# Gated linear attention in one kernel of two layers: chunks of 128 tokens with decays counted from the chunk's middle, in place of chunks of 64

## The reference

```python
def _gla_scan(q, k, v, log_a):            # chunks of c = 64 tokens, n = 4 of them
    cum = jnp.cumsum(log_a.reshape(b, h, n, c, dk), axis=3)
    q_t = q * jnp.exp(cum)
    k_t = k * jnp.exp(-cum)
    scores = jnp.where(mask, jnp.einsum('bhnid,bhnjd->bhnij', q_t, k_t), 0.0)
    o_inner = jnp.einsum('bhnij,bhnje->bhnie', scores, v)
    last = cum[..., -1:, :]
    kv = jnp.einsum('bhncd,bhnce->bhnde', k * jnp.exp(last - cum), v)
    decay = jnp.exp(last[..., 0, :])
    def step(state, inp):                 # state before a chunk, carried over the chunks
        kv_n, d_n = inp
        return d_n[..., None] * state + kv_n, state
    _, s_before = lax.scan(step, zeros, (kv, decay))
    o_cross = jnp.einsum('bhncd,bhnde->bhnce', q_t, s_before)
    return o_inner + o_cross
```

## Time and profile before

| | |
|---|---|
| time, median of 3 executions | 845.27 us (844.89 to 845.55) |
| span of the profiled execution | 843.8 us |
| median minus span | 1.5 us |
| PE busy | 829.3 us, 98% |
| PE weight loads | 701.4 us, 83% |
| DVE busy | 464.5 us, 55% |
| ACT busy | 428.4 us, 51% |
| DMA read | 147.85 MB, 178 GB/s over the span |

### The profile page before, as it was taken

The page is one execution under the profiler, slowest core; times in us unless marked ns, Lnnn a source line. Parts: engine busy times, 40 slices in busy tenths (PEclk is TensorE's granted clock), DMA queues, the critical chain, the costliest instruction groups (busy, mean ns, idle before and its releaser), DMA issues.

```text
span 843.8 us, 11480 instructions
## 1 busy us (share of the span) xinstructions
PE 829.3 (98%) x4084; PEld 701.4 (83%) x4084; DVE 464.5 (55%) x611; ACT 428.4 (51%) x616; POOL 50.2 (6%) x44
## 2 busy tenths in 40 slices
PE   6999999999999999999989999999999999999998
PEld 5898888888888888888869888888878888888886
DVE  2554497445375853654445635864653649546542
ACT  4864565456725543433347655663475345444441
POOL 6110000000000101000122000000000010010000
PEclk9999999999999999999989999999999999999999
DMA  8765764533543454565436656644354345546654
GB/s 343 251 230 190 240 215 150 174 125 126 175 150 125 147 178 150 193 206 198 156 117 227 246 186 227 198 150 150 125 175 147 128 147 162 176 139 204 194 186 140
DMA packets 41924, 150.67 MB, mean 179 GB/s; under 512 B 4752, under 2 KB 4880, under 8 KB 41744
## 3 DMA queue, kind: packets, MB, share of 16 engines
q1 hardware_dynamic: 40592, 145.25, 51.5%
q0 software_dynamic: 432, 2.88, 0.8%
q10 hardware_dynamic: 848, 1.83, 0.7%
HBM read 147.85 MB, written 2.10 MB: 178 GB/s over the span
## 4 chain that ended last, share of the span: by engine, by line
PE 96%; ACT 1%; issue 1%; DMA 1%; DVE 1%; SPq 0%; ACTq 0%; DVEq 0%
PE pair L357 84%; PE bank L388 4%; PE bank L637 1%; PE bank L611 1%; PE bank L500 1%; PE bank L679 1%; PE bank L669 1%; PE bank L592 1%; DMA raw<-stream 1%; PE bank L627 0%; PE bank L548 0%; PE bank L570 0%; PE bank L560 0%; ACT gate L731 0%; DVE lo L978 0%
## 5 line engine op out<-in xcount | busy, mean ns | idle before, releaser
L978 DVE TENSOR_TENSOR lo<-raw,hi 128x1024 fp32r<-128x1024 f32 (+3 forms) x266 | 307.3, 1178 | 213.1 <-ACT hi L713 209.2
L713 ACT ACTIVATE hi<-raw 128x1024 fp32r<-128x1024 f32 (+3 forms) x272 | 270.4, 1022 | 155.7 <-PE pair L357 132.5
L357 PE MATMUL pair<-lo,xT_hi 128*128 128x512 f32 (+1 forms) x768 | 296.9, 387 | 2.4 <-DVE xT_lo L995 2.4
L357 PE MATMUL pair<-hi,xT_hi 128*128 128x512 f32 (+1 forms) x768 | 296.0, 396 | 2.9 <-ACT xT_hi L747 2.6
L357 PE MATMUL pair<-hi,xT_lo 128*128 128x512 f32 (+1 forms) x768 | 296.9, 387 | 0.0
L357 PEld LDWEIGHTS pair<-lo,xT_hi 128*128 128x128 f32 x768 | 145.5, 189 | 30.2 <-issue 3.3
L357 PEld LDWEIGHTS pair<-hi,xT_hi 128*128 128x128 f32 x768 | 144.3, 189 | 30.4 <-ACT xT_hi L747 3.3
L357 PEld LDWEIGHTS pair<-hi,xT_lo 128*128 128x128 f32 x768 | 145.2, 189 | 28.5
L357 PE MATMUL pair<-hi,yT_hi 128*128 128x512 f32 (+1 forms) x304 | 116.7, 384 | 0.0
L357 PE MATMUL pair<-hi,yT_lo 128*128 128x512 f32 (+1 forms) x304 | 116.6, 383 | 0.0
L357 PE MATMUL pair<-lo,yT_hi 128*128 128x512 f32 (+1 forms) x304 | 116.5, 383 | 0.0
(11 more groups left out here) (138 smaller groups left out, 519.7 us busy)
## 6 DMA issues: line engine op xcount, KB each, us to landing
raw<-stream SPq DMA_DIRECT2D x272, 512.0 KB, 4.2
out<-x SPq DMA_DIRECT2D x8, 256.0 KB, 5.3
consts<-consts_in POOLq DMA_DIRECT2D x1, 1792.0 KB, 14.9
mats<-mats_in ACTq DMA_DIRECT2D x2, 576.0 KB, 3.5
x<-x_in POOLq DMA_DIRECT2D x2, 512.0 KB, 9.3
x<-x_in SPq DMA_DIRECT2D x1, 512.0 KB, 4.6
x<-x_in ACTq DMA_DIRECT2D x1, 512.0 KB, 9.0
consts<-consts_in ACTq DMA_DIRECT2D x1, 64.0 KB, 4.3
```

Source lines behind the costliest of these rows:

```text
L357: return nc.tensor.matmul(pair[a][m][:, 0:width], x_part[:, slots[i], m * P:(m + 1) * P], w_part[r][:, i * 512:i * 512 + width], start=(sl ...
L713: nc.scalar.activation(cut[0], cut[1], ACT.Copy).then_inc(rounded[r].sem, 1)
L978: nc.vector.tensor_tensor(cut[0], cut[1], cut[2].bitcast(F32), ALU.subtract).then_inc(split[r].sem, 1)
```

## The change

Mixer B works in chunks of 128 tokens, that is one chunk per token tile. The decays are counted from the middle of the chunk (token 64), not from its beginning, so that the exponents of q and k have both signs. In each direction only one state is left: what the first tile (of that direction) gives to the second. In detail:

- The triangular constants become `cum_f`, `cum_b` (signed sums around the middle), `keep_f`, `keep_b` (the masks), `after` and `before` over all 128 tokens, and a new one `halves` of 4 columns. The constants grow from 3584 to 3844 columns in the load that POOL issues.
- On PE the "rest of chunk" product is needed only for the tile that gives: 2 products of 256 columns where there were 4. New are 4 products of 2 columns (the decay from the tile's edge to its middle, `e_mid`).
- `k_dec` has no zeros beside blocks; a state update is 2 products of 256 columns per direction (heads in pairs): 4 where there were 16 of 128 columns, all at one place, where `outer_kv(0)` stood.
- The output of a tile is 4 products score by v and 4 products q by state with all 128 output rows, where there were 4 and 12 with 64 rows.
- ACT moves the state with 4 activations that scale by `e_mid`, where there were 12 copies; it evaluates 2 exponentials of 256 columns and 2 of 4 columns where there were 2 of 512.
- DVE makes `k_dec` in 2 instructions instead of 4; the 8 instructions that fold the state are gone. POOL no longer clears `k_dec`.

```diff
-                for m in range(MT):
-                    nc.tensor.matmul(bank[2 + m][:, 0:2 * P], const("after"), la[:, m, 0:2 * P],
+                for d, rest in enumerate(("after", "before")):
+                    gives, takes = d, 1 - d
+                    nc.tensor.matmul(bank[2 + d][:, 0:2 * P], const(rest), la[:, gives, d * 2 * P:(d + 1) * 2 * P],
                                      start=True, stop=True)
-                    nc.tensor.matmul(bank[2 + m][:, 2 * P:4 * P], const("before"), la[:, m, 2 * P:4 * P],
-                                     start=True, stop=True).then_inc(rem_filled.sem, 1)
+                    for f in range(2):
+                        at = d * 2 * P + f * P
+                        mm = nc.tensor.matmul(bank[2 + d][:, 2 * P + 2 * f:2 * P + 2 * f + 2],
+                                              la[:, takes, at:at + P], const("halves")[:, 2 * d:2 * d + 2],
+                                              start=True, stop=True)
+                    mm.then_inc(rem_filled.sem, 1)
...
                 pe.wait_ge(*v_b_ready.at(l, MT))
-                outer_kv(0)
-                granules(82)
-                outer_kv(1)
+                pe.wait_ge(*k_dec_ready.at(l, 2))
+                pe.wait_ge(*picked_ready.at(l, 2))
+                for d in range(2):
+                    for a in range(2):
+                        mm = nc.tensor.matmul(bank[2 + d][:, a * 2 * HD:(a + 1) * 2 * HD],
+                                              k_dec[:, d, a * P:(a + 1) * P],
+                                              v_b[:, d, a * 2 * HD:(a + 1) * 2 * HD], start=True, stop=True)
+                    mm.then_inc(kv_filled.sem, 1)
                 granules(85)
...
-                    for c in range(2):
-                        n = 2 * m + c
-                        for h in range(HEADS):
-                            for d in range(2):
-                                t = n - 1 if d == 0 else 2 - n
-                                if t < 0:
-                                    continue
-                                mm = nc.tensor.matmul(
-                                    bank[m][c * 64:(c + 1) * 64, h * HD:(h + 1) * HD],
-                                    q_heads[:, d, h // 2, m, h % 2, c * 64:(c + 1) * 64],
-                                    state[:, d, t, h // 2, :], start=False, stop=True,
-                                    skip_group_check=True)
+                    d = 1 - m
+                    for h in range(HEADS):
+                        mm = nc.tensor.matmul(
+                            bank[m][:, h * HD:(h + 1) * HD], q_heads[:, d, h // 2, m, h % 2, :],
+                            state[:, d, h // 2, (h % 2) * HD:(h % 2 + 1) * HD], start=False, stop=True,
+                            skip_group_check=True)
...
-                keep(0)
-                splits(84)
-                keep(1)
+                act.wait_ge(*e_mid_ready.at(l, 2))
+                for d in range(2):
+                    act.wait_ge(*kv_filled.at(l, d + 1))
+                    for a in range(2):
+                        nc.scalar.activation(state[:, d, a, :], bank[2 + d][:, a * 2 * HD:(a + 1) * 2 * HD], ACT.Copy,
+                                             scale=e_mid[:, d, a, 0:1]).then_inc(state_ready.sem, 1)
                 splits(84)
```

More of the change, by code:

```diff
@@ L84 @@
 CONSTS, nc_ = {}, 0
-for n_, w_ in (("ident", P), ("tri_f", P), ("tri_b", P), ("after", P), ("before", P),
+for n_, w_ in (("ident", P), ("cum_f", P), ("cum_b", P), ("keep_f", P), ("keep_b", P), ("after", P), ("before", P),
+               ("halves", 4),
                ("decay", HEADS * 3 * P), ("rcos", MT * HD // 2), ("rsin", MT * HD // 2),
@@ L177, in build @@
         sq_b = area(4096, 512)
-        e_rem = area(5120, 1024, "p (m d c) -> p m d c", m=MT, d=2)
+        e_rem = area(5120, 512, "p (d c) -> p d c", d=2)
         picked = area(7680, 512, "p (h i) -> p h i", h=HEADS)
-        state = area(6144, 1536, "p (d n a e) -> p d n a e", d=2, n=3, a=2)
+        state = area(6144, 1024, "p (d a e) -> p d a e", d=2, a=2)
+        e_mid = area(7168, 8, "p (d f o) -> p d f o", d=2, f=2)
         rq_rot = area(0, 1024, "p (n c) -> p n c", n=MT * HEADS)
@@ L590, in scores_b @@
                             pe.wait_ge(*e_rem_ready.at(l, d + 1))
+                            pe.wait_ge(*e_mid_ready.at(l, d + 1))
                         for f in range(2):
@@ L894, in _ @@
                 splits(76)
-                for m in range(MT):
-                    act.wait_ge(*rem_filled.at(l, m + 1))
-                    nc.scalar.activation(e_rem[:, m].rearrange("p d c -> p (d c)"), bank[2 + m][:], ACT.Exp,
+                for d in range(2):
+                    act.wait_ge(*rem_filled.at(l, d + 1))
+                    nc.scalar.activation(e_rem[:, d], bank[2 + d][:, 0:2 * P], ACT.Exp,
                                          scale=1.0 / GLA_TAU).then_inc(e_rem_ready.sem, 1)
+                    nc.scalar.activation(e_mid[:, d].rearrange("p f o -> p (f o)"), bank[2 + d][:, 2 * P:2 * P + 4],
+                                         ACT.Exp, scale=1.0 / GLA_TAU).then_inc(e_mid_ready.sem, 1)
                 splits(77)
@@ L902, in _ @@
                 splits(82)
[L904 to L915, removed]
-                                nc.scalar.activation(state[64 * i:64 * i + 64, d, t, :, :], cut[:, :, i, :], ACT.Copy
-                                                     ).then_inc(kv_kept.sem, 1)
-                keep(0)
-                splits(84)
-                keep(1)
+                act.wait_ge(*e_mid_ready.at(l, 2))
+                for d in range(2):
+                    act.wait_ge(*kv_filled.at(l, d + 1))
+                    for a in range(2):
+                        nc.scalar.activation(state[:, d, a, :], bank[2 + d][:, a * 2 * HD:(a + 1) * 2 * HD], ACT.Copy,
+                                             scale=e_mid[:, d, a, 0:1]).then_inc(state_ready.sem, 1)
                 splits(84)
@@ L1225, in _ @@
                 pick(1)
-                splits(82)
-                dve.wait_ge(*kv_filled.at(l, 2))
-                decay_k(1)
-                splits(84)
-                dve.wait_ge(*kv_kept.at(l, 12))
[L1232 to L1237, removed]
-                            nc.vector.scalar_tensor_tensor(
-                                out=state[:, d, t, a, :], in0=state[:, d, t - 1, a, :],
-                                scalar=e_pos[:, d, a, edge:edge + 1], in1=state[:, d, t, a, :],
-                                op0=ALU.mult, op1=ALU.add).then_inc(state_ready.sem, 1)
                 def head_squares(sq, m, squared, read):
@@ L1395, in shape_constants @@
     k, t = i[:, None], i[None, :]
-    same = (k // GLA_CHUNK) == (t // GLA_CHUNK)
     put("ident", k == t)
-    put("tri_f", same & (k <= t))
-    put("tri_b", same & (k >= t))
-    put("after", same & (k > t))
-    put("before", same & (k < t))
+    put("cum_f", 1.0 * ((k >= GLA_MID) & (k <= t)) - 1.0 * ((k < GLA_MID) & (k > t)))
+    put("cum_b", 1.0 * ((k < GLA_MID) & (k >= t)) - 1.0 * ((k >= GLA_MID) & (k < t)))
+    put("keep_f", k <= t)
+    put("keep_b", k >= t)
+    put("after", k > t)
+    put("before", k < t)
+    put("halves", np.concatenate([i[:, None] < GLA_MID] * 2 + [i[:, None] >= GLA_MID] * 2, axis=1))
     gamma = 1.0 - 2.0 ** (-5.0 - np.arange(HEADS))
```

49 lines of the change are left out of this document (16 added, 33 removed).

## The result

The changed kernel takes 834.7 us (834.22 to 834.93, 4 executions) against 845.25 (844.89 to 845.55, 4 executions) for the kernel before on the same chip. The ratio is 0.9882, 95% interval 0.987 to 0.9894. The forecast was 835.7.

The account below looks back on a forecast made before the run. PE was taken as the bound. From the 843.8 us span, -6.78 - 3.70 + 0.06 - 0.84 + 1.44 + 0.2 = -9.6 gave span 834.2, median 835.7 us; the 8-in-10 range was 833.3 to 838.0.

Parts of the forecast that it names:

- PE is the bound: Whole kernel: PE is busy 829.3 of 843.8 us, so PE time is kernel time unless PE must wait.
- Output products: Mixer B's output group on PE: falls from 6.96 to 3.57 us, -3.39 per layer, -6.78 in all.
- State updates: Mixer B on PE: two groups of 3.58 us become one of 1.73, -1.85 per layer, -3.70 in all.
- Rest of the chunk: Mixer B on PE: two wide products replaced by four 2-column ones at 0.224 us, +0.03 per layer, +0.06 in all.
- The old wait: Before granule 84: PE's wait for a late `lo` goes, -0.42 us per layer, -0.84 in all.
- The new wait: At granule 82: PE arrives before ACT's rounding, queued behind the state's move, is ready; +0.72 us per layer, +1.44 in all.
- One link: Within granule 82's wait: ACT starts its last two activations when direction 1 is filled, 1.92 us after the state update begins.
- Mixer B as a whole: All of mixer B's gains and losses taken together: -4.9 us per layer.
- The start: Kernel start: POOL's loads of x issued 0.95 us earlier compete with the first granule; +0.2 us, ends -0.3 and +0.5.
- such a microsecond: Start and layer boundary: the low-clock stretch's length may move by a microsecond with what stands before it.
- The reading that almost nothing of 64 rows runs side by side: Old output products: 64-row records cost 0.099 us each, against 0.056 by the skill's side-by-side rule.
- The rival of the clock: Mixer B: a longer wait at granule 82 lowers PE's clock in both layers, making the kernel slower, 849.1 us for example; chance 0.02.

Follow-up runs that it names:

- e1: Changed kernel with ACT's rounding of granule 82 placed ahead of the four activations that move the state: 833.15 us.
- e7: Changed kernel without its 2-column products, so the carried state has a wrong scale: 835.22 us.
- e3: Changed kernel with each 2-column product issued four times, 24 more in all: 844.8 us (838.98 to 846.93, 10 executions).
- e11: The same edit as e1, run beside the unedited changed kernel on one chip: 835.46 us against 835.25.
- e2: Changed kernel with half of `q_heads` cleared a second time before POOL's loads of x: 835.44 us.
- e9: Kernel before with 260 unused columns added to its constants: 845.61 us against 844.62, ratio 1.0008.
- e4: Changed kernel with each q by state product split into two of 64 output rows, upper and lower halves one behind the other: 836.9 us.
- e5: As e4, but the upper halves of all four heads first, then the lower ones: 838.52 us.
- e12: Kernel before with its 12 q by state products per tile reordered so neighbours lie in different halves where possible: 842.74 us against 844.62, ratio 0.9978.
- e6: Changed kernel with each state-update product cut into four of 64 moving columns, same weights: 838.78 us.

## Why the prediction was right

- *PE is the bound.* Held: 11.2 us less PE work gave a span shorter by 10.7.
- *Output products*, -3.39 per layer: 6.96 became 3.57. Held, because the same 32 records stood in mixer A.
- *State updates*, -1.85: 3.58 became 1.73 (251.46 to 253.19 in e1). Held.
- *Rest of the chunk*, +0.03: 1.74 in place of 1.73 (220.84 to 230.79, less 8.21 for the three granules). e7 gives 0.22 for one 2-column product, e3 0.21; 0.224 was taken. The rule of the Trainium skill (TensorE: Matmul & The Clock Gate, LDWEIGHTS), which gives 107 ns for 128 columns of weights, agrees with the 0.105 us a record of e3. The 0.2 us for all four, which the prediction worked out from its table for columns alone (Back-to-back issue gap), does not agree: they cost 0.87.
- *The old wait*, -0.42: gone, in both layers.
- *The new wait*, +0.72: 0.65. ACT's rounding of granule 82 began 2.65 us after the state update (254.02 less 251.37; forecast 2.72) and PE's granule 5.02 after it (5.10). e1 and e11 show that it is worth 0.68, and that it comes from the rounding's place on ACT. One link is not confirmed: the chain of the profile leads to the rounding from direction 0's filling through ACT's four activations, not from direction 1's. The two ways come out within 0.1 us of each other, so the number would be the same by either, and says nothing for the one that was drawn.
- *Mixer B as a whole*: -4.9 per layer forecast, -5.0 measured.
- *The start*, +0.2 in the sum: later by 0.16 at the first product and by 0.44 once the clock had risen. The sign was right and the reason wrong: not POOL's earlier loads (e2), but something that goes with the size of the constants (e9).
- *What was missing*: -1.2 at the beginning of layer 2, from a shorter low stretch; its cause is open. The prediction named such a microsecond without giving it a sign. Without it the spans would be 9.5 us apart, where the sum said 9.6. So the 1.0 us between 834.7 and the forecast is this stretch, and not a term of the sum; that the others add up this closely owes something to mixer B (0.2 more gained than forecast) and the start (0.2 more lost) cancelling.
- *The reading that almost nothing of 64 rows runs side by side*: right for the order that the kernel before has, wrong as a property of such products (e4, e5, e12). The sum rested on the measured 6.96 and not on it.
- *The rival of the clock*: did not happen in the changed kernel, where mixer B ran at 1.00 in the profile. But e3 shows that a fall inside a layer was nearer than its 2% suggests, and without any wait: it came behind added 2-column products.

## What to carry to other kernels

When a group of work is taken out of the bounding engine, look for what stood between it and the next wait: the saving moves the engine closer to its suppliers, and a supplier whose order still has the old step in front of the stream becomes late (here 0.65 us per layer, which a moved rounding gives back). The price of a new instruction is best taken from a row that shares its largest part (here the full weights, 0.224 us for 0.21 to 0.22 measured), not from a row with as many columns. Compare a change of a microsecond by stages in the profile, not by total times, when some stretch of the program varies by more.

## What the runs showed of the hardware that was not expected

- TensorE's clock can fall though the engine is never idle: behind 16 float32 products of 2 columns in 4.1 us it was at 0.51 for 3.4 us, and it fell at this place in both layers of the profile (e3), though one of ten executions had a mean clock of 1.0. Behind 16 products of 64 columns in 3.53 us it stayed at 1.00 (e6).
- Products of 64 output rows that go to different halves overlap when they are neighbours in program order: 0.064 us a record alternating, 0.094 in blocks (e4, e5), 0.079 when only the three products of a head alternate (e12). The change back to full width costs about 0.2 us (1.09 against 0.89).
- With full 128 x 128 weights a float32 product takes 0.21 to 0.22 us for 2, 64 and 128 columns alike (e3, e6).
